# A two-block transformer kernel: TensorE filled with matmuls of no use at five stage borders, and the mixer's group norm in another order

## The reference

```python
def first_block(x, c, ctx, c_ctx, ...):
    mod = (silu(c) @ ada_w + ada_b)            # shifts, scales and gates; the same for c_ctx
    x = macaron_ffn(x, mod[:, 0:3], *ffn1)
    ctx = macaron_ffn(ctx, mod_ctx[:, 0:3], *ffn1)
    h_ctx_f, h_ctx_b = context_states(ctx, ...)
    x, _, _ = mix_sublayer(x, mod[:, 3:6], h_ctx_f, h_ctx_b, *mix)
    return macaron_ffn(x, mod[:, 6:9], *ffn2)

def macaron_ffn(x, mod3, norm_pre, norm_post, w_gate, w_up, w_down):
    h = modulate(rms_norm(x, norm_pre), mod3[:, 0], mod3[:, 1])
    y = (silu(h @ w_gate) * (h @ w_up)) @ w_down
    return x + 0.5 * mod3[:, 2][:, None, :] * rms_norm(y, norm_post)
```

```python
    y = y.reshape(b, L, 768) * silu(z)
    y = rms_norm(y.reshape(b, L, 4, 192), ssd_norm.reshape(4, 192)).reshape(b, L, 768)
    out = concatenate([fourier_mix(u_f, fourier_w), y], axis=-1) @ w_out
    return x + mod3[:, 2][:, None, :] * rms_norm(out, norm_post), h_f, h_b
```

## Time and profile before

| | |
|---|---|
| Three runs, median (lowest to highest) | 3721.26 us (3715.21 to 3727.25) |
| The profiled execution, its own time | 3724.43 us |
| Its span, first to last instruction | 3723.1 us |
| Mean granted TensorE clock | 0.967 of 2.4 GHz |
| Busy share of the span | PE 94%, PEld 75%, DVE 45%, ACT 39%, POOL 38% |
| Chain that ended last | PE 76%, DVE 11%, ACT 5%, issue 3%, POOL 2%, DMA 2% |
| DMA | 376.45 MB, mean 101 GB/s |

### The profile page before, as it was taken

How to read it: one execution, slowest core, us unless ns; L and a number is a source line. 1 busy time by engine, 2 the same in 40 slices (tenths; PEclk the granted TensorE clock), 3 DMA queues, 4 the chain that set the end, 5 groups by cost and what they waited for, 6 DMA issues and landing times.

```text
span 3723.1 us, 45249 instructions
## 1 busy us (share of the span) xinstructions
PE 3510.5 (94%) x17424; PEld 2796.0 (75%) x17424; DVE 1672.8 (45%) x2997; ACT 1438.8 (39%) x2448; POOL 1428.4 (38%) x651
## 2 busy tenths in 40 slices
PE   6899999998799998999999999999998999999998
PEld 4788889785578886866676778887876766778886
DVE  7976463546420115845442243133754453234143
ACT  3223354554432223344443344343343443334342
POOL 3554433321244444334323444444333333344443
PEclk9999999999899998999999999999999999999999
DMA  7574355221122332212212222323222222223332
GB/s 300 193 248 145 126 160 166 69 86 51 46 74 91 102 91 81 90 62 82 78 64 91 86 79 89 103 90 110 82 72 71 71 74 89 76 85 95 98 95 81
DMA packets 118423, 376.45 MB, mean 101 GB/s; under 512 B 15424, under 2 KB 16320, under 8 KB 117952
## 3 DMA queue, kind: packets, MB, share of 16 engines
q1 hardware_dynamic: 107280, 356.33, 29.6%
q10 hardware_dynamic: 10928, 17.22, 1.6%
HBM read 359.86 MB, written 2.10 MB: 97 GB/s over the span
## 4 chain that ended last, share of the span: by engine, by line
PE 76%; DVE 11%; ACT 5%; issue 3%; POOL 2%; DMA 2%; ACTq 1%; SPq 0%; DVEq 0%; POOLq 0%
PE ps L1333 23%; PE ps L1334 22%; PE ps L1335 22%; DVE b L2194 2%; ACT b L1660 2%; PE ps L1576 1%; POOL b L2558 1%; PE ps L1597 1%; ACTq L1766 1%; PE ps L1558 1%; DVE b L2230 1%; PE ps L1631 1%; PE ps L1620 1%; PE ps L1554 1%; DVE b L2460 1%
## 5 line engine op out<-in xcount | busy, mean ns | idle before, releaser
L2558 POOL TENSOR_TENSOR b<-b,b 128x1024 fp32r<-128x1024 f32 (+2 forms) x579 | 1324.3, 2287 | 2183.2 <-ACT b L1660 2166.5
L1333 PE MATMUL ps<-b,b 128*128 128x512 f32 (+3 forms) x4848 | 1842.4, 380 | 75.1 <-POOL b L2558 29.2
L1334 PE MATMUL ps<-b,b 128*128 128x512 f32 (+3 forms) x4848 | 1803.4, 372 | 0.0
L1335 PE MATMUL ps<-b,b 128*128 128x512 f32 (+3 forms) x4848 | 1801.9, 372 | 0.0
L1333 PEld LDWEIGHTS ps<-b,b 128*128 128x128 f32 x4848 | 935.0, 193 | 309.7 <-issue 118.7
L1335 PEld LDWEIGHTS ps<-b,b 128*128 128x128 f32 x4848 | 934.1, 193 | 160.1
L1334 PEld LDWEIGHTS ps<-b,b 128*128 128x128 f32 x4848 | 935.4, 193 | 154.8 <-issue 5.1
L1660 ACT ACTIVATE b<-b 128x1024 fp32r<-128x1024 f32 (+2 forms) x622 | 607.4, 978 | 388.5 <-PE ps L1335 247.4
L2109 DVE SCALAR_TENSOR_TENSOR b<-ps,b,b 128x511 f32<-128x511 f32 x88 | 66.0, 750 | 365.0 <-ACT b L1711 365.0
L2194 DVE CUSTOM_DVE_ANT_0 b<-b,b,b 128x1024 bf16<-128x1024 f32 x112 | 218.7, 1953 | 16.1 <-DMA b<-in_ada 4.1
L1721 ACT ACTIVATE b<-b 128x512 fp32r<-128x512 f32 (+1 forms) x110 | 64.8, 590 | 397.4 <-DVE b L2118 294.7
(11 more groups left out here) (231 smaller groups left out, 2337.4 us busy)
## 6 DMA issues: line engine op xcount, KB each, us to landing
b<-in_w SPq DMA_DIRECT2D x458, 512.0 KB, 3.5
b<-in_ada SPq DMA_DIRECT2D x88, 512.0 KB, 5.2
b<-in_w SPq DMA_DIRECT2D x80, 384.0 KB, 3.1
b<-in_w SPq DMA_DIRECT2D x80, 320.0 KB, 2.9
b<-b ACTq DMA_DIRECT2D x176, 64.0 KB, 2.0
b<-in_const SPq DMA_DIRECT2D x24, 256.0 KB, 3.8
b<-in_x SPq DMA_DIRECT2D x1, 2048.0 KB, 16.4
out<-b SPq DMA_DIRECT2D x8, 256.0 KB, 2.5
```

What stands on the lines that cost most here:

```text
L1333: pe.matmul(out, a[0], b[0], start=first, stop=False)
L1334: pe.matmul(out, a[0], b[1], start=False, stop=False)
L1335: return pe.matmul(out, a[1], b[0], start=False, stop=last)
L2558: then(pool.tensor_tensor(wlo[j % NS][:, 0:nk * w], raw[j % NR][:, 0:nk * w], whi[j % NS][:, 0:nk * w].bitcast(F32), ALU.subtract), "lop", j)
```

## The change

Steps of a new kind, `idle`, are put into `S` at the five borders: TensorE multiplies the high part of the next stage's first weight chunk by itself (128 x 128 by 512) n times, into whichever rotating bank is next, and nobody reads the result. There are 8 ahead of a norm's last sum matmul (none for the plain norms), 12 behind it, and 3 behind each of the eight steps of `squares`. The five places are those of `addnorm(2)`, `squares(7)` and `prenorm(4)`; `addnorm(3)`, `squares(9)` and `prenorm(5)`; `prenorm(6)`, `prenorm(7)` and `prenorm(8)`. The group norm's steps are placed one by one in place of `groupnorm`, its sums use bank 6, and `yv` 5 stands ahead of the scaling of the second half's first tile.

```diff
@@ -319,17 +319,24 @@
     return dict(kind=kind, **kw)
-def prenorm(p):
+def prenorm(p, c=None):
+
+
     nid = PN[p]["norm"]
-    return [do("nfin", nid=nid)] + [do("pn", p=p, i=i) for i in range(8)] + [do("pnlow", p=p)]
-
-
-def addnorm(a):
-    return [do("nfin", nid=AN[a]["norm"])] + [do("an", a=a, i=i) for i in range(8)]
-
-
-def squares(nid):
-    return [do("nadd", nid=nid, i=i) for i in range(8)]
+    return (idle(c, 0 if nid in PLAIN else 8) + [do("nfin", nid=nid)] + idle(c, 12)
+            + [do("pn", p=p, i=i) for i in range(8)] + [do("pnlow", p=p)])
+
+
+def addnorm(a, c=None):
+    return (idle(c, 8) + [do("nfin", nid=AN[a]["norm"])] + idle(c, 12) + [do("an", a=a, i=i) for i in range(8)])
+
+
+def idle(c, n):
+    return [] if c is None or n == 0 else [do("idle", c=c, n=n)]
+
+
+def squares(nid, c=None):
+    return [x for i in range(8) for x in [do("nadd", nid=nid, i=i)] + idle(c, 3)]
 def schedule():
@@ -423,12 +430,9 @@
         F.step("fo3", m=m)
         F.spent(0.86)
-    def groupnorm(hf, o):
-
-        own = (0, 1) if o == 0 else (2,)
-        done = (0,) if o == 0 else (1, 2)
-        return ([do("gn1", hf=hf, o=x) for x in own] + [do("gn2", hf=hf, o=o), do("gn3", hf=hf, o=o)]
-                + [do("gn4", hf=hf, o=x) for x in done] + [do("gn5", hf=hf, o=x) for x in done])
+    def gnorm(hf, *steps):
+
+        return [do(kind, hf=hf, o=o) for kind, o in steps]
     sx, ss, hs = ([do(kind, d=y % 2, x=y // 2) for y in range(6)] for kind in ("sx", "ss", "hs"))
     scan = sx[:2]
@@ -448,9 +452,15 @@
         if 0 < h < 13:
             B, scan = B + [do("md", h=h - 1)] + scan[:3], scan[3:]
         if h % 2 == 0 and k > 0:
-            B += [do("yv", k=k - 1)] + (groupnorm(0, k - 2) if k in (2, 3) else [])
-            if k == 5:
-                B += groupnorm(1, 0)[:2]
+            B.append(do("yv", k=k - 1))
+            if k == 3:
+                B += gnorm(0, ("gn1", 0), ("gn1", 1), ("gn1", 2))
+            elif k == 4:
+                B += gnorm(0, ("gn4", 0), ("gn4", 1), ("gn4", 2), ("gn5", 0), ("gn5", 1), ("gn5", 2))
+            elif k == 5:
+                B += gnorm(1, ("gn1", 0), ("gn1", 1))
+        if h == 9:
+            B += gnorm(0, ("gn2", 0), ("gn3", 0), ("gn2", 1), ("gn3", 1))
     whole = F.begin("wo")
     tiles = [dict(name="wo", i=m, N=L, ver=("mix",), c=whole + m) for m in range(3)]
@@ -464,9 +474,12 @@
     S += weave(F, B, 1.5)
     F = fore()
     part(F, tiles[2], range(5))
+    S += gnorm(1, ("gn2", 0), ("gn3", 0)) + [do("yv", k=5)] + weave(F)
+    S += gnorm(1, ("gn1", 2), ("gn2", 1), ("gn3", 1), ("gn4", 0), ("gn5", 0))
+    F = fore()
     for t in tiles:
         part(F, t, range(5, 6))
-    S += weave(F, groupnorm(1, 0)[2:] + [do("yv", k=5)] + groupnorm(1, 1), 1.1)
+    S += weave(F) + gnorm(1, ("gn4", 1), ("gn4", 2), ("gn5", 1), ("gn5", 2))
     F = fore()
     for m, t in enumerate(tiles):
         if m > 0:
@@ -478,8 +491,11 @@
         t = F.fm("wo", m, "wo", ("mix",), L)
         F.step("evac", t=t)
         F.step("nadd", nid=6, i=m)
-    S += weave(F) + addnorm(2) + squares(7) + prenorm(4)
-    S += weave(ffn(2, "ffn2", ("pn", 4), L, 8)) + addnorm(3) + squares(9) + prenorm(5)
+    c = at[0]
+    S += weave(F) + addnorm(2, c) + squares(7, c) + prenorm(4, c)
+    F = ffn(2, "ffn2", ("pn", 4), L, 8)
+    c = at[0]
+    S += weave(F) + addnorm(3, c) + squares(9, c) + prenorm(5, c)
     for l in range(2):
         H = ("pn", 5 + 2 * l)
@@ -562,10 +578,10 @@
             t = F.fm("wo2", m, "wo2", ("mg", l), L, l=l)
             F.step("evac", t=t)
             F.step("nadd", nid=10 + 2 * l, i=m)
-        S += weave(F) + prenorm(6 + 2 * l)
+        S += weave(F) + prenorm(6 + 2 * l, at[0])
         S += weave(ffn(3 + l, "ffnb", ("pn", 6 + 2 * l), L, 11 + 2 * l, conv=l))
         if l == 0:
-            S += prenorm(7)
+            S += prenorm(7, at[0])
     S += [do("nfin", nid=13)] + [do("out", i=i) for i in range(8)]
     assert at[0] == len(stream)
     return S, stream
@@ -754,6 +770,8 @@
             mark("nrm", s["nid"], 7)
             mark("rs1", s["nid"])
             mark("rs", s["nid"])
+        elif k == "idle":
+            s["bank"] = brief()
         elif k == "pn":
             mark("pnq", s["p"], s["i"])
             mark("pnh", s["p"], s["i"])
@@ -872,11 +890,10 @@
         elif k == "gn1":
             mark("gs", s["hf"], s["o"])
         elif k == "gn2":
-            s["bank"] = gn_bank = take()
+            s["bank"] = 6
             mark("gp", s["hf"], s["o"])
         elif k == "gn3":
-            s["bank"] = gn_bank
-            held[gn_bank] = False
+            s["bank"] = 6
             mark("gl", s["hf"], s["o"])
             mark("ge", s["hf"], s["o"])
         elif k == "gn4":
@@ -1375,6 +1392,12 @@
                     pe.matmul(b[:, 0:N], ones, n_slot(nid, i if nid in PLAIN else 0)[:, 0:N], start=first,
                               stop=(i == 7)).then_inc(up("nrm", nid, i), 1)
                     freed[6 + nid % 2] = ("rs1", nid)
+            elif k == "idle":
+                w = whi[st["c"] % NS]
+                at.wait_ge(*n("hi", st["c"]))
+                b = bank_of(st["bank"])
+                for _ in range(st["n"]):
+                    pe.matmul(b[:, :], w[:, 0:128], w[:, 0:512], start=True, stop=True)
             elif k == "turn":
                 m = st["m"]
                 b = bank_of(st["bank"])
```

## The result

| | changed kernel | kernel before |
|---|---|---|
| Median of four runs each (lowest to highest) | 3702.97 us (3697.17 to 3704.01) | 3720.23 us (3715.21 to 3727.25) |
| Ratio, with its 95% interval | 0.9951 (0.9935 to 0.9967) | |
| The profiled execution | 3702.94 us, span 3701.6 | 3724.43 us, span 3723.1 |

A forecast was written before the change was run, and what follows sets the result against it. TensorE, busy 3510.5 of 3723.1 us, bounds the kernel; its waits and low clock can be won. Terms of -8.6, -4.9 and -2.6 sum to -16.1 us, giving a 3705 us median, range 3692 to 3717.

The forecast's parts named there:

- Term 1: Mixer's group norm up to the end of output block 5: reordering shortens waits and low clock, -8.6 us.
- the 2.0 for `z`'s bank: Mixer: new wait of the first Fourier sum for the bank of `z` tile 4, 2.0 us.
- the 1.2 of short ones: Mixer: three short new waits, on table transfers and block 2's first products, 1.2 us.
- the 0.9: Mixer: the second `fo3` waits for ScalarE, which does head 10's exponentials first, 0.9 us.
- the 0.5 + 2.3 for `fx`: Mixer: output-projection steps 0 and 1 wait for `fx` on VectorE, 0.5 and 2.3 us.
- Term 2: Group norm's second half: `yv` 5 goes ahead of tile 0's scaling, shortening the waits before input tile 6, -4.9 us.
- Term 3: The five borders: extra matmuls remove the low clock, but the third weight chunk limits the gain, -2.6 us.
- some 2.7 us at borders 2 and 4: Borders 2 and 4: TensorE's longer wait for the third weight chunk, some 2.7 us.
- (a): Mixer: the reordering gives only half, terms 1 and 2 at -4 and -3, median 3712 us; chance 0.22.
- (c): Borders: the fill doesn't hold the clock, about +31 us in place of -2.6, 3739 us; chance 0.05.
- (b): Borders: low clock is lost time, the third chunk no floor; term 3 -11.3, time 3696 us; chance 0.11.
- 3700.4: Whole kernel: the sum if half of all throttled time at the borders comes back, term 3 about -10.5 us.

The follow-up runs named there:

- The runs with 10.0: Profiles, reordering only and first half only among them, where output block 5's last matmuls start 9.9 to 10.0 us earlier than in the kernel before.
- both halves and one: Two kernels without fills, against the kernel before: the full group-norm reordering, 3707.53 us, and only its part up to output block 5, 3710.83 us.
- run 1: Changed kernel without any of the 172 extra matmuls, the group norm's new order alone; 3707.53 us, ratio 0.9959 to the kernel before.
- run 4: Changed kernel with 16 and 24 extra matmuls in place of 8 and 12, three per Square kept; 3714.78 us.
- The kernel with the constants later: Changed kernel without fills between Squares, ScalarE's constant loads at borders 2 and 4 issued behind the third chunk's rounding; 3697.53 us, then 3694.93 us.

## Why the prediction was right, and where it wasn't

**Term 1 (-8.6).** Right as a sum: block 5 ends 8.7 us earlier. Its split was off. The waits shrank by more than the 5.1 forecast: in the stretch up to block 5's end TensorE is idle 6.4 us (61.40 less 54.98) instead of 13.3, 6.9 less. Of the new waits the 2.0 for `z`'s bank measured 1.9, the 1.2 of short ones 1.2, the 0.9 0.7; the 0.5 + 2.3 for `fx` measured 1.8. The low clock gave less than the 3.5 forecast: busy time fell by 1.8. A wait of 0.7 us for a low part (L2413) was not in the list. The low clock holds 3.40 + 6.05 us of work now, with the first stretch right behind the new wait for `z`'s bank. The runs with 10.0 lack that stretch.

**Term 2 (-4.9).** Right: -6.0 in the changed kernel, -4.3 to -4.4 as the difference between both halves and one. Tile 5 was 2.7 us late (2.9 forecast), tile 6 0.5 (1.0), and TensorE reaches tile 6 12.6 us behind block 5. The 13 half-clock matmuls are gone (nine are left in run 1) and, as forecast, their place is taken by the wait for the fourth tile's weights, 2.1 us instead of 0.9.

**Term 3 (-2.6).** By border it was near: forecast -1.2, +0.3, -1.6, 0 and -0.1; where nothing else disturbs, -0.9, +0.3, -1.5, 0.0 and 0.0, which is -2.1 (the -1.6 of some profiles at border 4 is a later stretch of low clock, see the last section). The Ln of border 1 came 1.4 us later (1.1 forecast), and the sum of border 3 takes 1.12 us instead of 1.92. The step that failed is that nothing else of the program was counted. By the times the fills bring some 6 us, and by the profiles the further 3 to 4 stand at 1485 to 2156, which no row of the kernel before pointed to. The times can't place them: fills at borders 3 to 5 gave 5.3 us (3.3 by the ratio) and those at 1 and 2 1.4 (3.0), and neither can be told from none. The waits of "some 2.7 us at borders 2 and 4" were 1.6 and 1.7 (3.1 and 2.35 with a slow issue). The prediction had the path from the first product to the third chunk without a wait: in the changed kernel the weight loads wait there 1.2 to 1.3 us for the norm's tiles from GpSimd at borders 2 to 5, and not at all in the kernel before. So what the clock gave was taken up in part ahead of the chunk and in part by it.

**The rivals.** (a) fell: the mixer alone gives 14.4 to 14.7. (c) fell: the clock is 1.00 in every stretch filled as in the changed kernel. (b) fell as a mechanism: of the 20.9 us at half clock in the earlier trace rows none is left, and the borders gave 2.1; at border 5 3.1 us went and nothing was won. There the 48 matmuls from the first product to the third chunk took 12.47 us with 7 of them at half clock, and 12.45 us in the changed kernel, where waits of 1.3 us for the norm's tiles and 0.4 for the chunk stand in the place of the slow ones; without either it is 10.88 (run 4). A longer low start does cost: in the second profile of the kernel before, with 13, border 5 took 1.5 us more, and with the fills of the change it never did. The rule of the Trainium skill, "TensorE: Matmul & The Clock Gate", section "HAM oscillation", would give half of the throttled time back, which makes 10.5 us over the five and 1.5 at border 5 as an estimate. The traces disagree with 2.1 and 0.0: in the runs with the fills only the third chunk's first matmul came 0.3 us later at border 2 and no earlier at borders 4 and 5, and 1.0 and 1.6 earlier at 1 and 3. The kernel with the constants later shows it from the other side: at borders 2 and 4 more of the gain appears once the chunk comes earlier. (The 3700.4 that the prediction gives for the rule is the profiled execution's time; as a median, like its 3705, it would be 3697.2.)

**The time.** 3705 forecast, 3703 and 3699 measured; the differences are 17.3 and 19.6 us against a sum of 16.1. That it is so near is partly luck: terms 1 and 2 together were 1 us too small and term 3 some 3, and the interval of the measurement, 12 to 24 us, is wider than either.

## What to carry to other kernels

Price a stretch of low clock, and a gap, by what the engine waits for next: the gain ends at the next floor, here a weight chunk whose rounding stood behind four transfers' issues on ScalarE. Fills ahead of and behind a sum are free up to the gap's length and cost up to their own time beyond it, less where waits behind them take up a late start; between short dependent steps, where they fit least, they cost at once. Such fills can also change what comes later: here they move every later product to another bank. And compare two profiles of the same kernel before reading a difference of a few microseconds out of one of each.

## What the runs showed of the hardware that was not expected

The same stretch of one stage, with TensorE busy throughout, is at half clock for 13.7 us in one execution and 17.1 in another of the same kernel. Windows over it behind border 2, in the first and second profile of the kernel before, then in the changed kernel:

```profile
1457.35:1471.10 13.75, 13.75 (x58) 12.93 (x58) 9.57 (x12) 4.22 (x8) 9.91 (x5) 0.51 0.31 97
```

```profile
1455.95:1473.05 17.10, 17.10 (x69) 15.86 (x69) 11.17 (x19) 5.99 (x11) 10.27 (x5) 0.50 0.32 96
```

```profile
1441.40:1458.50 17.10, 17.10 (x69) 15.90 (x70) 11.11 (x18) 5.62 (x11) 10.27 (x5) 0.51 0.30 91
```

The longer one costs 1.7 us. It explains why border 2 reads +2.0 in four runs though the third chunk came only 0.3 late there, and why border 4 reads -1.6 in one profile of the fills and 0.0 in the other: the third chunk was on time in both, and the low stretch behind it lasted 13.7 us in one and 17.1 in the other.

The issue of one transfer on ScalarE took 1.87 us (1.15 in another run) where its neighbours took 0.45 (0.46 and 0.45 behind it). The third chunk's rounding stood behind it, and its first matmul came 1.4 and 0.7 us later for it.
